# The sample caches' shifted copy, cut in 45 pieces and spread over projection, attention and merging

## The reference, cut to what matters

```python
def dilated_group_sample(q, k_new, v_new, buf, window, dilation, slopes):
    wb = buf.shape[1]
    k_all = jnp.concatenate([buf[:, :, 0], k_new], axis=1)
    v_all = jnp.concatenate([buf[:, :, 1], v_new], axis=1)
    ...
    new_buf = jnp.stack([k_all[:, -wb:], v_all[:, -wb:]], axis=2)
    return o, lse, new_buf
```

## Time and profile before

| what | value |
|---|---|
| median of 3 runs | 1619.49 us (1618.11 to 1635.36) |
| the profiled execution, its own time | 1622.56 us |
| span of its instructions | 1620.7 us |
| granted TensorE clock, mean | 0.867 of full speed |
| busy, of the span: PE, PEld, DVE, ACT, POOL | 74%, 43%, 36%, 15%, 17% |
| moved by DMA | 455.44 MB, mean 281 GB/s |

### The profile page before, as it was taken

How to read it: one execution, slowest core, us unless ns; L and a number is a source line. 1 busy time by engine, 2 the same in 40 slices (tenths; PEclk the granted TensorE clock), 3 DMA queues, 4 the chain that set the end, 5 groups by cost and what they waited for, 6 DMA issues and landing times. The chain is left out here.

```text
span 1620.7 us, 14617 instructions
## 1 busy us (share of the span) xinstructions
PE 1204.8 (74%) x5502; PEld 699.6 (43%) x5502; DVE 587.9 (36%) x763; ACT 242.6 (15%) x393; POOL 280.2 (17%) x208
## 2 busy tenths in 40 slices
PE   4999999895699899843005997459878788777780
PEld 4878888784245444421004644423233233323230
DVE  2299999963543444350001213511011111111114
ACT  2121111002343343100000010011110101111112
POOL 1055555530033223000000000001101010101110
PEclk9999999998699989856557997579999999999995
DMA  6389989993567767665546405249999999999974
GB/s 197 131 297 340 328 304 335 362 351 118 232 253 287 277 234 275 225 251 202 213 207 231 166 0 211 118 161 410 408 410 404 407 410 401 411 403 407 404 282 175
DMA packets 99542, 455.44 MB, mean 281 GB/s; under 512 B 12768, under 2 KB 44816, under 8 KB 56832
## 3 DMA queue, kind: packets, MB, share of 16 engines
q1 hardware_dynamic: 73176, 300.09, 47.5%
q0 software_dynamic: 25776, 150.45, 24.9%
q10 hardware_dynamic: 544, 4.26, 0.7%
HBM read 442.10 MB, written 65.44 MB: 313 GB/s over the span
## 5 line engine op out<-in xcount | busy, mean ns | idle before, releaser
L423 PE MATMUL proj_ps<-hT,w_slots 128*128 128x260 f32 x1472 | 332.8, 387 | 8.5 <-ACT stage L446 6.1
L423 PEld LDWEIGHTS proj_ps<-hT,w_slots 128*128 128x128 f32 x1472 | 280.2, 192 | 58.9 <-issue 15.0
L1661 PE MATMUL ex_gp<-raw,ex_xT 128*64 128x512 f32 x1024 | 232.0, 601 | 21.3 <-DMA raw<-in_w_up_e 13.2
L1675 PE MATMUL ex_yp<-raw,ex_hmT 128*64 128x512 f32 x512 | 139.2, 693 | 69.0 <-DMA raw<-in_w_down_e 68.5
L209 POOL DMA_INDIRECT ring<-in_cache_k_a,run_sb x64 | 138.9, 2171 | 192.5 <-DVE scores L481 164.3
L474 DVE TENSOR_TENSOR ring<-ring,q_rep 128x2048 f32<-128x2048 f32 x64 | 145.9, 2281 | 41.1 <-ACT q_rep L465 41.1
L481 DVE TENSOR_REDUCE scores<-ring 128x32 f32<-128x2048 f32 x64 | 145.8, 2280 | 0.0
L1661 PEld LDWEIGHTS ex_gp<-raw,ex_xT 128*64 128x64 f32 x1024 | 70.6, 138 | 158.8 <-issue 123.7
L1180 PE MATMUL mg_ps<-oT,mg_wb 128*128 128x260 f32 x192 | 45.0, 399 | 125.2 <-DMA mg_wb<-in_w_br_b 125.2
L1616 DVE TENSOR_TENSOR ex_hm<-ex_sg,ex_gp 64x512 f32<-64x512 f32 x32 | 21.7, 680 | 267.5 <-ACT ex_sg L1596 267.5
L209 POOL DMA_INDIRECT ring<-in_cache_v_a,run_sb x64 | 73.4, 1146 | 255.7 <-PE at_vp L695 240.4
(11 more groups left out here) (239 smaller groups left out, 1063.3 us busy)
## 6 DMA issues: line engine op xcount, KB each, us to landing
raw<-in_w_gate_e SPq DMA_DIRECT2D x64, 1024.0 KB, 21.6
raw<-in_w_up_e SPq DMA_DIRECT2D x64, 1024.0 KB, 27.5
raw<-in_w_down_e SPq DMA_DIRECT2D x64, 1024.0 KB, 26.0
o_kvs<-in_cache_kv_b SPq DMA_DIRECT2D x1, 32752.0 KB
w_slots<-in_w_in SPq DMA_DIRECT2D x23, 1024.0 KB, 8.5
o_kvs<-in_cache_kv_b SPq DMA_DIRECT2D x1, 8176.0 KB
kv<-in_cache_kv_b SPq DMA_DIRECT2D x24, 256.0 KB, 6.0
gate_rows<-stage SPq DMA_DIRECT2D x16, 260.0 KB, 8.7
```

The source lines that it names most:

```text
L423: last = pe.matmul(pp[:, j, half, 0:H], w[:, m % 2, c, j * P:(j + 1) * P], k.hT[:, c, half * H:(half + 1) * H], start=(c == 0), stop=(c == ...
L1661: last = pe.matmul(gp[at:at + SLOT, j], xT[:, c, :], raw[:, slot, c1 * FF:(c1 + 1) * FF], start=(c == 0), stop=(c == KC - 1))
L1675: last = pe.matmul(yp[h * SLOT:(h + 1) * SLOT, j], hmT[:, c, :], raw[:, slot, o:o + 512], start=(c == 0), stop=(c == FC - 1))
```

## The change

The copy is cut into 45 pieces. A piece takes 64 rows (the last one of each group but for its remnant takes 60), as 16 chunks of 4 rows (one run of 8 KB) for each of 8 samples, with the chunks as the outermost dimension; the last 3 rows of each group are a piece of their own, 8 samples x 6 KB. A full piece moves 1.05 MB. The pieces are issued by SP in three places:

- 22 pieces in `project` (20.94 MB): 5 at the head of the block, then one behind each of the weight loads m = 2 to 18.
- 8 pieces in `attend` (8.39 MB): one at the head, then one when each of samples 0 to 6 has had its values used (SP waits for the ring).
- 15 pieces in `merge` (14.66 MB), behind all of the `mg_wb` loads and after SP has waited for `mg_wo` and `x`.

The copies in `weigh_a` and `decode_b` are gone. SP's loop over the `mg_wb` loads is written out without a loop register. The final wait counts 45 pieces.

```diff
+SHIFT_RUN = 4
+
+def shift_pieces():
+    out = []
+    for g, (wlen, _) in enumerate(GROUPS):
+        whole = (wlen - 1) // SHIFT_RUN * SHIFT_RUN
+        for at in range(0, whole, SHIFT_PIECE):
+            out.append((g, at, min(SHIFT_PIECE, whole - at)))
+        out.append((g, whole, wlen - 1 - whole))
+    return out
+
+def shift(k, eng, pieces):
+    for g, at, n in pieces:
+        r = SHIFT_RUN if n % SHIFT_RUN == 0 else n
+        v = lambda ap: ap.rearrange("b (n r) e -> n b (r e)", r=r)
+        eng.dma_start(v(k.io[f"o_kvs{g}"][:, at:at + n, :]),
+                      v(k.io[f"cache_kv_b{g}"][0].rearrange("b w k h d -> b w (k h d)")[:, at + 1:at + 1 + n, :]))\
+            .then_inc(k.shifted, 16)
+
+SHIFT_PIECE = 16 * SHIFT_RUN
+IN_PROJECT = 22
+IN_ATTEND = DEC
...
+                pieces = shift_pieces()[:IN_PROJECT]
+                early = IN_PROJECT - (N // 2 - 2 - 4)
+                shift(k, sp, pieces[:early])
                 for m in range(2, N // 2):
                     sp.wait_ge(s["made"], 2 * m - 2)
                     load_w_in(k, sp, m)
+                    if 2 <= m < 2 + len(pieces) - early:
+                        shift(k, sp, pieces[early + m - 2:early + m - 1])
...
                 sp.dma_start(k.tables_b[:], k.io["consts"][:, k.at["rel"][0]:k.at["row_bias"][0]]).then_inc(tables_in, 16)
-                for g in range(NG - 1):
-                    shift(k, sp, g)
                 sp.wait_ge(tables_in, 16)
...
+            @block.sync
+            def _(sp):
+                for b in range(DEC):
+                    if b:
+                        used_all(sp, b - 1)
+                    shift(k, sp, shift_pieces()[IN_PROJECT + b:IN_PROJECT + b + 1])
...
                         sp.dma_start(k.kv[:, b, g, :], k.io[f"cache_kv_b{g}"][0, b].rearrange(
                             "(n d) k h e -> n d (k h e)", d=d)[:, 0, :]).then_inc(kv_in, 16)
-                shift(k, sp, NG - 1)
...
-                with sp.Fori(0, TRIPS) as i:
+                for i in range(TRIPS):
                     for j in range(BUFS):
...
+                sp.wait_ge(wo_in, 16)
+                sp.wait_ge(x_in, 32)
+                shift(k, sp, shift_pieces()[IN_PROJECT + IN_ATTEND:])
...
-                    sp.wait_ge(k.shifted, 16 * NG)
+                    sp.wait_ge(k.shifted, 16 * len(shift_pieces()))
```

More of the change, by code:

```diff
@@ L489, in _ @@
                 reduce(N_GROUPS - 1)
[L492 to L497, removed]
 def weigh_a(k):
@@ L1104, in _ @@
             def _(sp):
-                with sp.Fori(0, TRIPS) as i:
+                for i in range(TRIPS):
                     for j in range(BUFS):
-                        sp.wait_ge(s["yb"], i * BUFS + (j + 1))
-                        at = i * (BUFS * P) + j * P
+                        t = i * BUFS + j
+                        sp.wait_ge(s["yb"], t + 1)
                         sp.dma_start(wb[:, j, 0:CA], k.io["w_br_a"][0].rearrange("(c p) n -> p c n", p=P)[
-                            :, :, bass.ds(at, P)]).then_inc(w_in[j], 16)
+                            :, :, t * P:(t + 1) * P]).then_inc(w_in[j], 16)
                         sp.dma_start(wb[:, j, CA:CA + CB], k.io["w_br_b"][0].rearrange("(c p) n -> p c n", p=P)[
-                            :, :, bass.ds(at, P)]).then_inc(w_in[j], 16)
+                            :, :, t * P:(t + 1) * P]).then_inc(w_in[j], 16)
+                sp.wait_ge(wo_in, 16)
+                sp.wait_ge(x_in, 32)
+                shift(k, sp, shift_pieces()[IN_PROJECT + IN_ATTEND:])
             @block.scalar
```

## The result

The changed kernel takes 1511.16 us (median of 4 runs, 1509.2 to 1513.14) against 1619.38 us before (4 runs): a ratio of 0.932, with a 95% interval of 0.926 to 0.937. The prediction was 1512 us in a range of 1500 to 1557. The profiled execution has its own time of 1509.2 us and a span of 1507.3 us, 113.4 us less than the span before.

What follows compares the result with a forecast made beforehand. The prediction took PE's busy projection and its 125.2 us idle before merging, behind group 2's copy in SP's queue, as what matters: 1622.56 - 116.4 - 1 + 10 = 1515.2 us, or 1512 us against the median, range 1500 to 1557.

Steps and rivals of the forecast that it cites:

- Merging's wait: Head of merging: with no copy ahead of the `mg_wb` loads, PE's idle time falls from 125.2 to about 8.8 us, -116.4.
- Decoding, and the stretch beside `weigh_a`: Decoding: -1 us, between 0 and -3; stretch 390 to 440: two small copies go, nothing waits for a transfer, 0.
- The projection: Projection with 22 pieces, 20.94 MB: +10 us in sum, with +4 and +19 as its ends.
- capacity: Projection, 80 to 300 us: 13.6 MB of pieces against room for 12.5 MB at 384 GB/s, +3 us.
- weight loads: Projection: weight loads share engines with gathers and pieces, and 6 us of cover does not always suffice, +2 us.
- gate stores: Projection: gate stores behind m = 17 and 18 stand behind a piece each, lengthening the wait of ACT and PE, +5 us.
- Merging's pieces and the router: Merging: 15 pieces, 14.66 MB, fit in the 76.6 us before the router's first load, 0 us.
- if a byte of the copy costs the DMA engines as much as a loaded byte: Projection's capacity step: copied bytes weigh like loaded ones, so 1.1 MB are too many, 3 us.
- Attention: Attention: 8 pieces want 22 us of 71 us of free engines, 0 us; bound 8 x 1 us.
- Rival 1: The copy path, not the engines, stands at 212 GB/s, so pieces count double: projection +44, 1546 us; chance 0.30.
- Rival 2: Pieces, reading samples 4 MB apart, run at 106 GB/s: projection +125, router's loads +62, 1689 us; chance 0.05.
- Rival 3: Pieces are free in the projection: gathers are late, DVE's cover takes all, gate store +1 us, 1503 us; chance 0.10.

Runs made afterwards that it cites:

- f2: Changed kernel with the 17 pieces behind the projection's weight loads issued in attention instead, five staying at the projection's head; 1509.57 us, 0.932 of before.
- e1: Changed kernel with the projection's 22 pieces left out, so 20.94 MB are not copied; 1504.09 us, 0.928 of before.
- e3: Kernel before with group 2's single 33.5 MB transfer, uncut, moved behind merging's loads; 1599.13 us, 0.986 of before.
- e4: Kernel before with group 2's copy cut into 33 pieces of 16 chunks at its old place in `decode_b`; 1584.43 us, 0.977 of before.
- e5: Changed kernel with merging's share cut into pieces of 8 chunks, so 8 DMA engines carry them in 8 KB runs; 1509.42 us.
- e6: Changed kernel with merging's bytes moved in two large transfers and a remnant, in runs of 64 and 46 KB; 1508.70 us.
- f3: The changed kernel unaltered, run again beside two other experiments; 1511.21 us, 0.933 of before.
- e7: Changed kernel with merging's 15 pieces moved into the projection too, 35.6 MB there in all; 1555.17 us.
- g1: Kernel before with only the two gate stores of m = 17 moved ahead of the other stores; 1612.95 us, 0.996 of before.
- e8: Changed kernel with the pieces behind m = 17 and 18 issued at attention's head and the first two gate stores ahead of other stores; 1497.37 us, 0.924.
- e2: Changed kernel with the pieces behind m = 17 and 18 issued at attention's head, old store order kept; 1509.52 us, 0.931 of before.
- f1: Changed kernel with all pieces in place and only the two gate stores of m = 17 moved ahead of other stores; 1510.49 us, 0.933.

## Why the prediction was right

**Merging's wait.** Predicted -116.4, measured -119.1 for the wait and -119.6 for the stage. The mechanism held: no copy ahead, PE starts on the first landed load. The term was undersized by 3 us. I took the landing of 7.3 us from a median that the copy itself had raised; undisturbed it is 3.7 to 4.1.

**Decoding, and the stretch beside `weigh_a`.** Predicted -1 and 0. Decoding measured +0.4. Attention with that stretch measured -2.2, but over the 13 kernels other than f2 it varies by 6 us, e1 among them at 289.3; these single traces tell no effect from none.

**The projection.** Predicted +10 as 3 (capacity) + 2 (weight loads) + 5 (gate stores), ends +4 and +19; measured +7.6. Five kernels have no piece behind a weight load of the projection and the old order of stores (before, e1, e3, e4, f2); their stage ends at 389.0 to 394.8, 390.9 on average. Four have the change's projection (after, e5, e6, f3): 395.8 to 397.8, 396.7 on average. So the pieces cost 6 us there, and the 7.6 of a single pair holds some chance. By the parts: PE's wait for `stage` is 6.0 to 10.6 us in the five, 7.5 on average, and 11.1 to 13.6 in the four, 12.9 on average: +5.4 where I had 5 (the pair alone gives 13.3 - 6.1 = +7.2). The capacity term was the wrong step; it measured nothing. I had taken 384 GB/s as the room of the mixture, but e7 reaches 408 to 410, and g1 against e8 shows 20 pieces at 0.1 us. The weight loads measured 0.2 us in after, 3.5 in f3 and none in e5 and e6, 0.9 on average, where I had 2. So the sum of +10 was 2 us above the pair and 4 above the averages, and the capacity term is most of it.

**Merging's pieces and the router.** Predicted 0, in 38 us at 384 GB/s or 69 at 212. They take 49 us at 298, between the two, and the cost was 0. My step "if a byte of the copy costs the DMA engines as much as a loaded byte" holds in the mixture (408 GB/s in e7, 407 without copies in the experts' stage); a copy alone with 16 engines costs 408/298 = 1.4 times as much.

**Attention.** Predicted 0 with 8 pieces; the rows agree, and f2 shows where it ends: 25 pieces cost 4 to 5 us in its one trace against the average of the others (289.1).

**The sum.** 1512 against 1511.16 is closer than the terms were, and that is in part luck. Between the two profiled executions the gain is 113.4 us, 6 more than my 107.4, with misses of 1 to 3 us in merging, decoding, attention and projection; between the medians it is 108.2.

**Rival 1** (a ceiling of 212 GB/s on the copy's path, 1546 us) fell: the ceiling is there, but at 298. The trace of before really could not tell: in e5 8 engines again give 215, in a kernel whose 16 give 298. The Trainium skill's page "DMA: Bandwidth & Descriptors", section "Latency and other measured facts", calls 214 GB/s, for each direction, full rate for copies between HBM tensors; here 8 KB runs on 16 engines moved 298, and the measurement decides.

**Rival 2** (half the rate from the 4 MB between samples, 1689 us) fell by the same row: 298 GB/s at that distance. **Rival 3** (free pieces, 1503 us) missed by 8 us, of which the gate stores are 5 to 7; e8 shows that 20 of the 22 pieces can be free once the gate stores come first, though not by the mechanism I named. I had thought that DVE's slack would absorb late gathers. The gathers are hardly late: DVE waits for them for 1.9 us in all, even in e7.

**What stays open.** Why the issue of a gate store lasts 9 us behind a piece, and still 4.9 in g1, without any piece. That SP is held until earlier transfers of its queue have moved on fits with the 94.06 us of the earlier trace rows and the 90.16 of e3. It is not the bytes alone: merging's 14.66 MB are issued in 19.23 us as 15 pieces, in 50.68 as e5's 29 and in 1.96 as e6's three transfers. Whether the number of transfers or of runs decides, no run tells. Open is also whether merging could take pieces from the projection's end as well; 27 us were free there, and it wasn't tried.

## What to carry to other kernels

A large transfer that nobody waits for still has a price: it is paid by whatever is issued behind it in the same queue, so look there, and check after a move who is next in that queue (e3: 119 us won, 97 given back). Cutting it so that all DMA engines share each piece, and moving it behind the loads that someone waits for, need each other (36 and 22 us alone, 108 together with the spreading over three stages). Pieces in a busy stage were nearly free here, as long as none stood ahead of a store whose slot someone waits for and that store was issued early itself; 35.6 MB in the projection were too many (e7). When a wait has two causes in a row, undoing either alone can show next to nothing; run both alone and together (e2, f1, e8) before one of them is ruled out.

## What the hardware showed that I had not expected

- A copy from HBM to HBM alone: 8 engines 215 GB/s (26.9 each), 16 engines 298 with runs of 8 KB (18.6 each) and 324 with runs of 46 to 64 KB. The busy share reads 1.00 and 0.98 in the two 16-engine cases, so it does not say how much more could be moved. With loads in the mixture 16 engines moved 410.
- With all engines full for 270 us (e7) POOL's indirect gathers cost DVE no more waiting (1.9 us) than in the change, while the loads of SP's queue, in which the pieces stood, landed in 17.3 us rather than 9.6. The lateness stayed in the queue that had the pieces; how the engines divide themselves between queues, these runs do not tell.
